# Second block's down projections: eight of 22 feature tiles by seven block products

## What is computed

```
D_FF_2 = 2816

def swiglu(x, w_gate, w_up, w_down):
    return (jax.nn.silu(x @ w_gate) * (x @ w_up)) @ w_down

def second_block(...):
    for l in range(DEPTH_2):
        h = h + 0.5 * swiglu(rmsnorm(h, ffn1_norm[l]), ffn1_w_gate[l], ffn1_w_up[l], ffn1_w_down[l])
...
        h = h + 0.5 * swiglu(rmsnorm(h, ffn2_norm[l]), ffn2_w_gate[l], ffn2_w_up[l], ffn2_w_down[l])
```

## Time and profile before

| | us |
|---|---|
| median of 3 runs | 3073.48 (3073.17 to 3073.59) |
| the profiled execution | 3072.61 |
| its span, first to last instruction | 3070.9 |
| the four down stages in it | 128.2, 128.1, 128.1, 122.0 |

### The profile page before, as it was taken

The page is one execution under the profiler, slowest core; times in us unless marked ns, Lnnn a source line. Parts: engine busy times, 40 slices in busy tenths (PEclk is TensorE's granted clock), DMA queues, the critical chain, the costliest instruction groups (busy, mean ns, idle before and its releaser), DMA issues.

```text
span 3070.9 us, 55350 instructions
## 1 busy us (share of the span) xinstructions
PE 3037.0 (99%) x20274; PEld 2756.7 (90%) x20274; DVE 2031.1 (66%) x3004; ACT 1411.5 (46%) x2481; POOL 170.9 (6%) x213
## 2 busy tenths in 40 slices
PE   8999999999999999999999999999999999999998
PEld 7778886888888799999999999999999999889986
DVE  5545545773576588855667788747885576788864
ACT  4454434442343365633752455425553365255541
POOL 1000000000000011100000011001110000001100
PEclk9999999999999999999999999999999999999999
DMA  4111322222222267532111477235762321157622
GB/s 160 62 63 62 110 90 94 92 96 96 96 96 95 77 159 183 141 103 96 63 63 63 130 184 180 91 103 165 178 154 93 100 70 64 68 142 191 170 103 103
DMA packets 121793, 341.30 MB, mean 111 GB/s; under 512 B 13774, under 2 KB 13774, under 8 KB 121536
## 3 DMA queue, kind: packets, MB, share of 16 engines
q1 hardware_dynamic: 97776, 292.33, 28.3%
q0 software_dynamic: 23600, 46.87, 9.0%
q10 hardware_dynamic: 288, 0.31, 0.0%
HBM read 337.29 MB, written 2.17 MB: 111 GB/s over the span
## 4 chain that ended last, share of the span: by engine, by line
PE 72%; issue 23%; DVE 2%; ACT 1%; DVEq 1%; POOL 1%; DMA 0%; POOLq 0%; ACTq 0%; SPq 0%
PE ps L2142 30%; PE ps L2244 9%; PE ps L2505 8%; PE ps L2502 8%; PE ps L2503 8%; PE ps L2787 3%; PE ps L2261 1%; PE ps L2329 1%; PE ps L2568 1%; PE ps L2189 1%; PE ps L2222 0%; PE ps L2298 0%; PE ps L2317 0%; PE ps L2170 0%; DVE w_lo L1306 0%
## 5 line engine op out<-in xcount | busy, mean ns | idle before, releaser
L700 ACT ACTIVATE w_hi<-w_raw 128x1024 fp32r<-128x1024 f32 x352 | 372.7, 1059 | 782.1 <-PE ps L2142 559.4
L1306 DVE TENSOR_TENSOR w_lo<-w_raw,w_hi 128x1024 fp32r<-128x1024 f32 x360 | 440.0, 1222 | 343.1 <-ACT w_hi L700 337.5
L2142 PE MATMUL ps<-f_hi,w_hi 128*128 128x264 f32 (+1 forms) x1488 | 383.8, 315 | 0.0
L2142 PE MATMUL ps<-f_lo,w_hi 128*128 128x264 f32 (+1 forms) x1488 | 383.3, 315 | 0.0
L2142 PE MATMUL ps<-f_hi,w_lo 128*128 128x264 f32 (+1 forms) x1488 | 382.4, 314 | 0.0
L2142 PE MATMUL ps<-h_hi,w_hi 128*128 128x512 f32 (+1 forms) x832 | 273.7, 357 | 0.3 <-DVE w_lo L1306 0.2
L2142 PE MATMUL ps<-h_lo,w_hi 128*128 128x512 f32 (+1 forms) x832 | 273.8, 357 | 0.0
L2142 PE MATMUL ps<-h_hi,w_lo 128*128 128x512 f32 (+1 forms) x832 | 272.6, 356 | 0.0
L2142 PEld LDWEIGHTS ps<-f_hi,w_hi 128*128 128x128 f32 x1488 | 244.3, 188 | 18.8
L2142 PEld LDWEIGHTS ps<-f_hi,w_lo 128*128 128x128 f32 x1488 | 244.0, 188 | 18.3
L2142 PEld LDWEIGHTS ps<-f_lo,w_hi 128*128 128x128 f32 x1488 | 244.8, 188 | 17.3
(11 more groups left out here) (409 smaller groups left out, 7490.5 us busy)
## 6 DMA issues: line engine op xcount, KB each, us to landing
w_raw<-in_stream SPq DMA_DIRECT2D x436, 512.0 KB, 3.3
s_raw<-in_stream SPq DMA_DIRECT2D x152, 256.0 KB, 4.4
s_raw<-in_stream POOLq DMA_DIRECT2D x152, 256.0 KB, 4.2
tmp<-in_stream SPq DMA_DIRECT2D x76, 256.0 KB, 5.2
xT<-in_x POOLq DMA_DIRECT2D x1, 2048.0 KB, 8.8
out<-tmp SPq DMA_DIRECT2D x8, 256.0 KB, 2.1
xT<-in_x SPq DMA_DIRECT2D x7, 256.0 KB, 5.7
const<-in_const POOLq DMA_DIRECT2D x1, 1636.0 KB, 9.0
```

The costliest lines, as they stand in the source:

```text
L700: nc.scalar.activation(w_hi[:, s, :], w_raw[:, s, :], ACT.Copy).then_inc(hi_done, 1)
L1306: V.tensor_tensor(w_lo[:, s, :], w_raw[:, s, :], w_hi[:, s, :].bitcast(F32), ALU.subtract).then_inc(lo_done, 1)
L2142: last = T.matmul(out[:, p, :], w[:, s, j * P:(j + 1) * P], x[:, k, c0:c1], start=start and j == 0 and r == 0, stop=stop and j == len(ks) ...
```

## The change

The first two output tiles stay plain, but their units come in another order: feature tiles 0 to 7 for both, then 16 to 21 for both, then 8 to 15. The other six tiles are made in three pairs. In a pair, feature tiles 8 to 15 (two blocks of four) against the two output tiles and the two token halves are a 2 x 2 x 2 block product, done by seven products on 12 matmuls each. Each pair takes seven units: P0, P1, P2 (48 matmuls, plain), W (a product and four plain blocks, 36 matmuls), and A, S, Q (two products, 24 matmuls). Their order in each pair is given by `D_ORDER`. A, S and Q read weights from `w_mix`, whose sums are formed by two adding DMAs of the GpSimd queue and two additions on DVE. Four sums of the features (d_sum, split to d_hi and d_lo in the place of h_hi and h_lo) are formed once a stage. Products that several outputs share go through banks 6 and 7 and are copied to `cp`, a part of tmp. The loops over tiles are written out.

```diff
+D_ORDER = {1: ["P0", "P1", "P2", "W", "A", "S", "Q"],
+           2: ["P0", "P1", "A", "S", "Q", "W", "P2"],
+           3: ["A", "S", "Q", "W", "P0", "P1", "P2"]}
...
+D_FIRST_PAIR = [(0, range(0, 8)), (1, range(0, 8)), (0, range(16, 22)), (1, range(16, 22)),
+                (0, range(8, 16)), (1, range(8, 12)), (1, range(12, 16))]
...
+        def d_banks(which, L, p):
+            a, b = ffn2_banks(which, L)
+            return {1: (4, a), 2: (b, 4), 3: (a, b)}[p]
...
+                def mixed_loads(p):
+                    sp.dma_start(w_mix[:, 0, :], stream_d[unit_of(2 * p + 1, 1), :, BLK:]).then_inc(s1_base[1], 16)
+                    sp.dma_start(w_mix[:, 3, :], stream_d[unit_of(2 * p, 1), :, 0:BLK]).then_inc(s3_base[1], 16)
+                    sp.dma_start(d_mixed("A"), stream_d[unit_of(2 * p, 1), :, :]).then_inc(wg_in[1], 16)
...
+                    elif kind == "W":
+                        sp.dma_start(w_raw[:, s, 0:BLK], stream_d[unit_of(2 * p + 1, 1), :, BLK:]).then_inc(w22_in[1], 16)
+                        sp.dma_start(w_raw[:, s, BLK:], stream_d[unit_of(2 * p + 1, 2), :, 2 * P:6 * P]).then_inc(w_arrived[s], 16)
...
+                for p in range(1, D_PAIRS + 1):
+                    for d in range(7 * p, 7 * p + 7):
+                        if d == d_at(p, "A"):
...
+                            d_copy_out(0, 6)
+                        if d == d_at(p, "S"):
...
+                            d_copy_out(3, 7, -1.0)
+                        if d == d_at(p, "Q"):
+                            act.wait_ge(unit_done, down + d + 1)
+                            d_copy_out(2, 6, -1.0)
+                        d_next(d)
+                        if p == D_PAIRS and d == d_at(p, "W") and not last:
+                            for k in range(2 * D_PAIRS):
+                                act.wait_ge(slot_free[k % 2], g0 + FF2_TILES + k // 2 + 1)
+                                h_upper(q, k, q + 2, T2)
+                if not last:
                     for s in range(2):
-                        down_tile(i, s)
+                        act.wait_ge(slot_free[s], g0 + FF2_TILES + D_PAIRS + 1)
+                        h_upper(q, 2 * D_PAIRS + s, q + 2, T2)
...
+                def d_out(p, s):
+                    y = tmp[:, 2, 0:n_tok]
+                    base = d_banks(which, L, p)[s]
+                    V.tensor_tensor(y.rearrange("p (a n) -> p a n", a=2), ps[:, base:base + 2, 0:hn], cp[:, 2 * s:2 * s + 2, :],
+                                    ALU.add)
+                    dve.drain()
+                    V.tensor_tensor(y, y, rstd[:, 0:n_tok], ALU.mult)
+                    dve.drain()
+                    take(2 * p + s, y)
...
+                d_t_sums()
+                for k in range(16, 22):
+                    f_lower(k)
+                d_next(0)
...
+                d_next(5)
+                first_out(0)
+                d_next(6)
+                first_out(1)
...
+                        for s in range(2):
+                            ends = max(d_at(p, "Q"), *(d_at(p, D_CLOSE[p][n]) for n in (("bw", "by"), ("bz", "bq"))[s]))
+                            if d == ends:
+                                dve.drain()
+                                dve.wait_ge(unit_done, down + d + 1)
+                                d_out(p, s)
+                        if p == D_PAIRS and d >= 7 * p + 5:
+                            d_next(d)
...
+                        if i == 0:
+                            pe.wait_ge(slot_free[1 if p > 1 else 0], g0 + FF2_TILES + (p - 1 if p > 1 else 1))
+                            pe.wait_ge(slot_free[0], g0 + FF2_TILES + p)
+                            pe.wait_ge(t_lo_done, 8 * z + 8)
```

More of the change, by code:

```diff
@@ L1065, in last_pair @@
                     down_upper(1)
-                    for k in range(7, 9):
+                    for k in range(7, 8):
                         f_upper(k)
@@ L1101, in ffn2 @@
                 q = 3 + 3 * L + 2 * which
[L1103 to L1115, removed]
@@ L1802, in ffn2 @@
                 V.memset(sumsq[:, :], 0.0)
+                dve.sem_inc(win_lo, 6 * D_PAIRS)
                 q = 3 + 3 * L + 2 * which
[L1805 to L1811, removed]
-                    for n in range(2):
-                        next_low(n)
-                        if first and n == 0:
-                            for k in range(16, FF2_TILES):
-                                f_lower(k)
-                    dve.wait_ge(unit_done, 2 * (u0 + FF2_TILES) + 6 * i + 3 * s + 3)
-                    x = tile(xT, 2 * i + s, n_tok)
+                down = 2 * (u0 + FF2_TILES)
@@ L1819, in down_tile, with first_out @@
+                def first_out(s):
+                    dve.wait_ge(unit_done, down + (7 if s else 5))
                     y = tmp[:, 2, 0:n_tok]
@@ L1821, in down_tile @@
                     dve.drain()
-                    V.scalar_tensor_tensor(x, y, 0.5, x, ALU.mult, ALU.add).then_inc(slot_free[s], 1)
-                    new_x(q, 2 * i + s, x, n_tok, last)
-                    next_low(2)
-                down_tile(0, 0, first=True)
-                down_tile(0, 1)
-                with dve.Fori(1, KT // 2) as i:
-                    for s in range(2):
-                        down_tile(i, s)
+                    take(s, y)
+                d_t_sums()
+                for k in range(16, 22):
+                    f_lower(k)
@@ L2540, in ffn2, with first_unit, f_ready @@
-                down_tile(0, 0, first=True)
-                down_tile(0, 1)
-                with pe.Fori(1, KT // 2) as i:
-                    for s in range(2):
-                        down_tile(i, s)
+                down = 2 * (u0 + FF2_TILES)
+                def first_unit(d):
+                    m, ks = D_FIRST_PAIR[d]
+                    def f_ready(k):
+                        pe.wait_ge(al_done, a0 + f_place(k) + 1)
+                    unit(u0 + FF2_TILES + d // 2, d % 2, bank(at_bank[m], n_tok), f2_hi, f2_lo, ks, n_tok,
+                         start=ks[0] == 0, stop=ks[-1] == 2 * KT - 1, step=f_ready)
@@ L2546, in mixer @@
+                for p in range(1, D_PAIRS + 1):
+                    d_pair(p)
             def mixer(L):
```

308 lines of the change are left out of this document (266 added, 42 removed).

## The result

The changed kernel takes 3143.7 us (median of 4 runs, 3143.1 to 3144.8) against 3073.5 us. The ratio is 1.0229, with a 95% interval of 1.0216 to 1.0242: 2.3% slower. The forecast was 3136 us with a range of 3112 to 3150.

What follows compares the result with a forecast made beforehand. PE, busy 99%, was taken as the bound. To 3072.6 us came three stages of +11.9 each, the last +10.4 and 17 for the clock: 3135.7; with the median 0.9 above the profiled run, 3136 us, range 3112 to 3150.

Steps and rivals of the forecast that it cites:

- The clockwork of a unit: Down-stage units: weights for the unit after next ready 2.63 us after a unit's start; 24-matmul units (2.93 us) fit by 0.3.
- Wait 1: PE idle before a down stage's third unit, behind DVE's feature sums and lowerings: 2.9 us, 3.1 in the last stage.
- wait 2: PE idle before pair 1's first unit, which waits for slot_free 0: 1.2 us, 1.3 in the last stage.
- Wait 4: PE idle before pair 3's Q, whose w_lo stands behind five output operations on DVE: 1.9 us a stage.
- wait 5: End of stage: tile 6's h_hi and h_lo delay the next stage 4.7 us; last stage only 0.8 us in the tail.
- wait 3: PE idle before pair 2's first unit until the output of the unit just finished is in xT: 5.3 us a stage.
- The other added work is covered: Down stages: sums, copies, w_mix loads, late h_hi and h_lo cost nothing at this pace; uncovered, each 0.4 to 4 us.
- rival (d): Half loads for W land late: 1.4 us at W, 1.4 in wait 3; about 3150 us, chance 0.14.
- The clock: After 11 waits longer than 2.44 us, PE runs 3.1 us at half speed, losing 1.55 us each: 17 us in all.
- rival (a): Waits come as computed, but the low clock falls into the idling and is over when matmuls resume: 3119 us, chance 0.20.
- Rival (b): DVE and ACT run ahead or waits hide in others: half of the 62 us, less their clock; about 3090, chance 0.08.
- (c): Faster: PE waits nowhere for output or weights, all five releases coming early: 3059 us, chance 0.03.

Runs made afterwards that it cites:

- the fastest kernel: Changed kernel with all five waits taken away, plus part of tile 6's and 7's outputs added to xT earlier, while DVE idled: 3061.7 us, ratio 0.9961 to the kernel before.
- The first run: Changed kernel, but the first units of pairs 1 and 2 no longer wait for slot_free 0; their second unit does: 3114.0 us.

## Why the prediction was right

**What bounds the kernel, and what is removed.** Right. Once PE does not wait, the stages last 124.5 to 125.3 and 121.0 us; computed were 124.0 and 120.0. Of the 14.4 us the down stages of the fastest kernel save 10.4; 3 of the missing 4 us are pauses of 0.1 to 0.5 us and slow first matmuls behind them, most of them at the product units.

**The clockwork of a unit.** Right to 0.1 us: w_lo begins 1.57 us after the end of Q in the changed kernel, computed 1.64. The fit of 0.3 us held in the units where nothing stands in front.

**Waits 1, 2, 4 and 5.** Computed 2.9, 1.2, 1.9 and 4.7 us; measured in the first stage 3.0, 1.3, 1.9 and 4.7. In the last stage waits 1, 2 and 4 were computed at 3.1, 1.3 and 1.9 us and read 3.3, 1.4 and 2.0. Waits 1 and 5 each went away alone when their order was undone, and wait 2 went together with wait 3. Wait 4 was taken away only on top of the others, and with it went the two small pauses ahead of A and S.

**Wait 3** was sized at 5.3 us and measured 5.8, 5.4, 6.1 and 5.4. Part of the excess is the same everywhere: PE restarted 0.3 us after the end of the last operation on xT, not 0.05. The rest differs by stage. In the first stage the chain of 0.79 us was broken once, and from the second to the third operation it took 1.15 us:

```profile
1377.46 1.23 DVE L1462 TENSOR_TENSOR w_lo<-w_raw,w_hi 128x1024 fp32r<-128x1024 f32 x1 [0.51 <-ACT w_hi L811]
1378.78 0.71 DVE L2006 TENSOR_TENSOR tmp<-ps,tmp 128x528 f32<-128x528 f32 x1
1379.56 0.71 DVE L2009 TENSOR_TENSOR tmp<-tmp,rstd 128x528 f32<-128x528 f32 x1
1380.71 0.71 DVE L2000 SCALAR_TENSOR_TENSOR xT<-tmp,xT 128x528 f32<-128x528 f32 x1 [0.44 <-issue]
```

In the other three it went at 0.77 to 0.79 us. In the third stage, the longest, the weights came late. Behind Q, ACT makes w_hi for pair 2's second unit (P1), and DVE makes its w_lo ahead of the eviction. This w_hi waited 0.44 us for its load, so that w_lo began 2.1 us after the end of Q and not 1.6:

```profile
2416.22 1.06 ACT L811 ACTIVATE w_hi<-w_raw 128x1024 fp32r<-128x1024 f32 x1 [0.44 <-DMA w_raw<-in_stream]
```

**The other added work is covered.** Right while the waits were there, since a wait of 5.8 us covers much. The first run showed that with wait 3 gone the outputs and A's sums on DVE cost 0.7 to 0.8 us twice a stage. The longer work on the last output showed behind the stage once wait 5 was gone. The half loads landed soon (the group holds W's and those of the first pair):

```profile
w_raw<-in_stream SPq DMA_DIRECT2D x384, 512.0 KB, 3.4
...
w_raw<-in_stream SPq DMA_DIRECT2D x32, 256.0 KB, 2.7
```

They landed in 2.7 us in the median, not in 5.2, and PE has no pause at W. So rival (d) is wrong about W. Its other half, a late load inside wait 3, did happen in one stage of four, with some 0.5 us and not 1.4, and for P1's load, not for W's.

**The clock.** Sized at 17 us, all of it after waits 1, 3 and 5. The mechanism was right, its places were not quite: after wait 1 the clock fell in the first two stages only, and it fell after wait 4 (1.9 and 2.3 us) in the first two too, to which I had given nothing. From the spacing of the matmuls the low clock costs 14 us inside the stages and 6 us in the first matmuls behind them, 20 in all: 4.3, 6.6 and 5.9 us after waits 1, 3 and 5, where 6.2, 6.2 and 4.7 were computed, and 3.1 after wait 4. That the first three come so near 17 together is in part luck, since the terms were off both ways. The idle matmuls in those three waits took 17.0 us away, and with that rival (a) fell. The advice of the Trainium skill (TensorE: Matmul & The Clock Gate, "Why this matters for your kernels") to stay below gaps of about 3 us is not safe here: pauses of 1.9 and 2.3 us were followed by half speed. One reading of the earlier trace rows needs a word: the row of the program's start has a granted clock of 1.00 and does not itself show a low one. That PE was slow there is seen from its count, 7 matmuls of 512 columns in 3.07 us, 0.43 us each, against the 0.23 us of the last stage.

**The sum.** Measured are 62.9 us of waits in the stages, 20 us of clock, -14.4 us of matmuls and 1.2 us at both ends of the program, 69.7 us; the difference of the medians is 70.2. Computed were 59.6 us of waits in the stages and 0.8 in the tail, 17 us of clock and the same -14.4. Of the 7.7 us that the forecast was short, 3.3 are waits (half of that wait 3) and 3 are clock, which is wait 4's share. Half a microsecond is rounding: 3135.7 and 0.9 are 3136.6, noted as 3136. Rival (b) speaks of 62 us of waits where the terms add to 60.4. Rivals (b) and (c) are refuted by the trace: no wait hid another, and none came early.

## What to carry to other kernels

When one engine is busy 99% of the time, an algorithm that saves it 0.5% is decided by the order in which the others prepare its operands, so write down the chain behind each of its restarts, in the order of the program, before counting what is saved. Put a wait at the first instruction that needs it and not at the head of the group: here moving such a wait by one unit gave 30 us. Before adding work to an engine "ahead" of a deadline, look whether the engine is idle there in the trace; the same two operations cost 4.3 us in one place and, one unit earlier and done for two tiles, gained 5.6 us.

## What the runs showed of the hardware

The granted clock does not follow a gap's length alone. PE idle for 3.0 us ahead of the third unit: half speed after it for 6.8 and 3.4 us in the first two stages, none in the third and fourth, in one execution. Idle for 1.9 us ahead of pair 3's Q: half speed in the first stage, none in the third. Every low stretch in and right behind the down stages was 3.4 or 6.8 us long. Filling a wait with idle matmuls kept the clock at 1.00 without shortening the wait, and was worth 15 to 17 us; one of them costs 0.86 us for 512 columns of plain float32, where a matmul of the kernel's own products on rounded halves takes 0.23 us.
